# Moving the first steps of an attention between the last products of a Fourier stage

## The chip, the cores and the metric

The kernel runs on one core of one Trainium2 chip. The metric is the device time of one execution in microseconds (us), and lower is better. The engines are PE (TensorE, the matrix engine), ACT (ScalarE), DVE (VectorE), POOL (GpSimd) and SP, which only issues loads here. Each engine works through its own instructions in the order in which the program lists them, and waits for the others by semaphores.

## The reference, cut to what matters

The model is one block with a Fourier branch beside an attention branch, followed by a second block (retention, latent attention, feed-forward). The change touches only the end of the Fourier branch and the beginning of the first attention. What they compute is this:

```
def fourier_branch(f_in, w_fmix, b_fmix):
    f = f_in.reshape(b, l, 8, 64)
    fr = real(fftn(f, axes=(1, 3), norm='ortho'))
    return einsum('blgc,gcd->blgd', fr, w_fmix) + b_fmix     # times silu(f_gate)

def gqa_block(q_blk, k, v):
    s = einsum('bkgqd,bksd->bkgqs', q_blk, k) * HEAD_DIM ** -0.5
    p = softmax(s, axis=-1)
    return einsum('bkgqs,bksd->bkgqd', p, v)                 # times silu(a_gate)
```

There are 1024 tokens and 16 meta tokens (1040 keys), 8 query heads of 64 values and 2 key and value heads.

## The kernel before, in words

**Where the work lies.** PSUM, the memory into which PE writes, is used as four pairs of banks, A, B, C and Dp (the trace calls them psa, psb, psc and psd). A pair holds 2 x 512 values for each of 128 partitions. Tiles in the other on-chip memory stand at addresses that are written out by hand, so a tile may reuse the place of another that is dead.

**The Fourier stage** (`pe_fourier`, `act_fourier`, `dve_fourier`). It has two steps. First come five small blocks of 8 matmuls ("mixed"), which ACT copies to the tiles GA and GB. ACT then also makes the high parts of the keys for both heads (KHH), and DVE the low parts (KLL), since a float32 operand is worked on as a high and a low part. Then come eight products, called "four" 0 to 7, of 20 matmuls with 260 columns each (L793). Behind product n, ACT copies one of its two banks to QSB (`L816`), and DVE does four operations (L832, L837, L838, L842): it forms the difference and the sum of both banks in PSB and multiplies each into the gate tile GT. L832 and L838 read one operand from PSUM and one tile of the other memory; L837 and L842 read two tiles of the other memory. The products go round all four pairs.

**The first attention** (`pe_attention`, `act_attention`, `dve_attention`, `pool_attention`). It works on 64 units, u = 0 to 63, of 128 queries of one head against all keys; four units make a group g. Before the loop stand five steps that are done once: the values are turned to tokens x channels by 9 transposes into pairs C and Dp (`pe_values_in`, L858 and L859), ACT copies them to the tile VS1 as high parts and DVE forms the low parts (signal "v low"); DVE splits the first queries (`dve_stage_first`, L877 and L879, signal ("q", 0)); PE computes the scores of the first group against the 16 meta tokens into pair Dp (`pe_meta_scores`, 8 matmuls of 16 columns), ACT copies them out and DVE takes their maxima; and PE computes the scores of unit 0 (`pe_scores`, four matmuls of 512 columns into pair A; unit u uses pair A or B in turn). Then, for each unit, DVE takes the maximum over the keys (L1054) and makes the bias (L1056), ACT computes the exponentials (L991, then L995 for the meta tokens), DVE inverts the sum (`dve_norms`, L1062 and L1065), POOL multiplies the probabilities by it (L1106, L1107), PE turns them by 8 transposes into pair C (`pe_turns`, L940), ACT and DVE split these into high and low parts (PTH and PTL, L1004 and L1071), and PE multiplies them with the values, once for each group, into pair Dp (L962). The turning lags three units behind the scores. On PE the order of a step u is: turns of u-3, scores of u+1, a third of a group's value matmuls, and after every fourth unit the next group's meta scores. POOL also splits the next head's queries (L889 and L897, signal ("q", n)) and gates each group's output (L1136).

**What orders the work around the change.** The order on each engine is written out: `tensor_program` calls `pe_gate`, then `pe_fourier`, then `pe_attention`, and the other engines have the same sequence. The attention's one-time steps therefore wait for product 7 and for its last DVE operation: `pe_values_in` waits for ("four", 7), `act_values_in` for ("four gated", 7). POOL has nothing between its last weight split and unit 0.

Of the kernel before, what the change touches and what calls it, by code (L numbers as in the profile page):

```python
# [6 lines left out]
F32 = mybir.dt.float32  # L7
F32R = mybir.dt.float32r
# [105 lines left out]
def two_block_kernel(nc, xT, pT, pos, slabs, cols, squares, rope1, dft, wf, cd, outT):  # L114
    with ExitStack() as ctx:
# [53 lines left out]

        PTH = [at(f"pth{j}", [P, 8, HALF], F32R, 27 + 32 * j) for j in range(2)]  # L170
        PTL = [at(f"ptl{j}", [P, 8, HALF], F32R, 43 + 32 * j) for j in range(2)]
        PM = [at(f"pm{j}", [P, 4, META], F32, 91 + 0.25 * j) for j in range(2)]
        KHH = [at(f"khh{j}", [P, L], F32R, 137.5 + 8.25 * j) for j in range(2)]
        KLL = [at(f"kll{j}", [P, L], F32R, 141.625 + 8.25 * j) for j in range(2)]
        PMS = [at(f"pms{j}", [P, 4, 2 * META], F32R, (91.5, 203.5)[j]) for j in range(2)]
        PMX = [at(f"pmx{j}", [P, 4, 2 * META], F32, (91.5, 203.5)[j]) for j in range(2)]
        PMT = at("pmt", [2 * META, HALF], F32R, 108.5)
        VS1 = [at(f"vs1{j}", [P, 9, P], F32R, 92 + 4.625 * j) for j in range(2)]
        QST = [at(f"qst{j}", [P, T], F32R, (199, 101.25)[j]) for j in range(2)]
# [114 lines left out]
        def col(name, j=0, lo=0, hi=P):  # L294
            return COLS[lo:hi, COL[name] + j:COL[name] + j + 1]
# [448 lines left out]
        def dve_fold(e):  # L744
# [12 lines left out]
            t.then_inc(*vec.up("wbd"))  # L757

        def four_pair(n):
            return (A, B, C, Dp)[n % 4]  # L760

        def fourier_free(e, n):

            if n >= MT5 + 4:
                e.wait_ge(*vec.on(("four", n - 4 - MT5)))
            elif n >= 4:
                e.wait_ge(*acted.on(("mixed", n - 4)))
            elif n == 0:
                e.wait_ge(*vec.on(("gate", 7)))
                e.wait_ge(*vec.on("wbd"))  # L770

        def pe_fourier(e):
            for mt in range(MT5):
                w = min(P, NM - mt * P)
                p = four_pair(mt)
                fourier_free(e, mt)
                for a, F_ in enumerate((FE, FO)):
                    for ct in range(4):
                        t = e.matmul(PS[p][0:w, a, ct * P:ct * P + P], lhsT=F_[:, ct, mt * P:mt * P + w],
                                     rhs=WBD[:, a, ct, :], start=True, stop=True, skip_group_check=True)  # L780
                t.then_inc(*psum.up(("mixed", mt)))
            e.wait_ge(*acted.on(("mixed", MT5 - 1)))
            e.wait_ge(*landed["ct"].on("all"))
            e.wait_ge(*landed["st"].on("all"))
            for n in range(8):
                dt, h = divmod(n, 2)
                p = four_pair(MT5 + n)
                fourier_free(e, MT5 + n)
                c0, cn = h * (NL // 2), NL // 2
# [8 lines left out]
        def act_fourier(e):  # L798
            e.wait_ge(*vec.on(("gate", 7)))
            for mt in range(MT5):  # L800
                w = min(P, NM - mt * P)
                e.wait_ge(*psum.on(("mixed", mt)))
                e.activation(GA[0:w, mt, :], PS[four_pair(mt)][0:w, 0, :], ACT.Copy)
                e.activation(GB[0:w, mt, :], PS[four_pair(mt)][0:w, 1, :], ACT.Copy).then_inc(*acted.up(("mixed", mt)))
            for kv in range(2):
# [4 lines left out]
                e.activation(KHH[kv][rest, :], K1[mine, :], ACT.Copy).then_inc(*acted.up(("k both", kv)))  # L810
            for n in range(8):
                cn = NL // 2
                e.wait_ge(*psum.on(("four", n)))
                if n >= 1:
                    e.wait_ge(*vec.on(("four", n - 1)))
                e.activation(QSB[:, 0:cn], PS[four_pair(MT5 + n)][:, 1, 0:cn], ACT.Copy  # L816
                             ).then_inc(*acted.up(("four", n)))

        def dve_fourier(e):
            for kv in range(2):  # L820
# [3 lines left out]
                e.tensor_tensor(KLL[kv][rest, :], K1[mine, :], KHH[kv][mine, :], SUB).then_inc(*vec.up(("k low", kv)))  # L824
            for n in range(8):
                dt, h = divmod(n, 2)
                c0, cn = h * (NL // 2), NL // 2
                p = PS[four_pair(MT5 + n)]
                k0 = META - 1 if h == 0 else 0
                k1 = cn if h == 0 else cn - 1  # L830
                e.wait_ge(*acted.on(("four", n)))
                e.scalar_tensor_tensor(out=PSB[:, 0:cn], in0=p[:, 0, 0:cn], scalar=col("b_fmix", dt), in1=QSB[:, 0:cn],  # L832
                                       op0=ADD, op1=SUB).then_inc(*vec.up(("four minus", n)))
                r0 = c0 + 1 + k0 - META
                seg = GT[:, dt, r0:r0 + cn - k0]
                e.wait_ge(*vec.on(("four minus", n)))
                e.scalar_tensor_tensor(out=seg, in0=PSB[:, k0:cn], scalar=0.5, in1=seg, op0=MUL, op1=MUL)  # L837
                e.scalar_tensor_tensor(out=PSB[:, cn:2 * cn], in0=p[:, 0, 0:cn], scalar=col("b_fmix", dt),  # L838
                                       in1=QSB[:, 0:cn], op0=ADD, op1=ADD).then_inc(*vec.up(("four", n)))
                seg = GT[:, dt, T - (c0 + k1):T - (c0 + 1) + 1]  # L840
                e.wait_ge(*vec.on(("four", n)))
                e.scalar_tensor_tensor(out=seg, in0=PSB[:, cn + k1 - 1:cn - 1:-1], scalar=0.5, in1=seg,  # L842
                                       op0=MUL, op1=MUL).then_inc(*vec.up(("four gated", n)))

# [10 lines left out]
        def pe_values_in(e):  # L855
            e.wait_ge(*vec.on(("four", 7)))
            for kt in range(8):
# [3 lines left out]
        def act_values_in(e):  # L861
            e.wait_ge(*psum.on("v turned"))
            e.wait_ge(*vec.on(("four gated", 7)))
            for kv in range(2):
# [2408 lines left out]
```

## Time and profile before

| what | us |
|---|---|
| median of three runs | 2178.56 (2178.27 to 2182.41) |
| the profiled execution | 2179.39 |
| its span in the trace | 2177.6 |
| products 0 to 7, PE | 270.4 to 311.8 |
| the attention's one-time steps and first units until the first turning | 311.8 to 331.5 |
| the rest of the attention's units | 331.5 to about 555 |

Times of the trace count from the start of its span. A row of the timeline gives the start, the duration, the engine, the line of the kernel, the operation, what is written and what is read, and, in brackets, how long the engine had been idle before it and what released it. PEclk and the granted clock are the clock that TensorE was given, as a share of its full 2.4 GHz; 0.50 is the lower of its two levels, 1.2 GHz.

### The profile page before, as it was taken

To read this page: it belongs to the slowest core of one execution; us is meant where nothing else is said; L and a number is where in the kernel's file an instruction comes from. 1 tells how busy PE (TensorE), PEld (TensorE's weight loads), DVE (VectorE), ACT (ScalarE), POOL (GpSimd) and SP (SyncE) were. 2 spreads that over 40 slices of the span, in tenths; PEclk is the share of its full clock that TensorE was granted. 3 is DMA by queue.
4 is the path that set the end of the run, shared out by engine and by line. 5 is a ranking of instruction groups with operands and counts; after the bars stand their busy time and mean duration, and the time that the engine had idled before them with its cause. 6 is when DMAs were issued, how large, how long until landed. Compare 5 with 4: busy or idle time off the path is not lost.

```text
span 2177.6 us, 25594 instructions
## 1 busy us (share of the span) xinstructions
PE 1992.6 (92%) x9543; PEld 1638.3 (75%) x9543; DVE 1322.9 (61%) x1846; ACT 917.1 (42%) x1614; POOL 941.9 (43%) x658
## 2 busy tenths in 40 slices
PE   5999988999999999988888798789999999999878
PEld 5987757777778888866766686667888887787667
DVE  5354148998786354455545546577655568969735
ACT  4121217888532222245556544443333343445541
POOL 0333308888000000007566100479999995746030
PEclk9999989999999999989999999899999999999989
DMA  3112100000423111100000231323232238784202
GB/s 146 49 39 90 47 0 1 1 1 1 145 87 135 40 39 39 40 20 30 20 20 20 97 96 59 135 87 107 81 113 88 91 122 295 233 303 164 87 30 97
DMA packets 68412, 179.57 MB, mean 82 GB/s; under 512 B 6529, under 2 KB 8321, under 8 KB 68289
## 3 DMA queue, kind: packets, MB, share of 16 engines
q1 hardware_dynamic: 42624, 120.19, 16.9%
q10 hardware_dynamic: 25664, 57.74, 7.3%
q8 instruction: 77, 1.26, 0.3%
q14 instruction: 47, 0.38, 0.1%
HBM read 148.02 MB, written 29.88 MB: 82 GB/s over the span
## 4 chain that ended last, share of the span: by engine, by line
PE 28%; DVE 11%; issue 6%; ACT 5%; POOL 4%; DMA 0%; ACTq 0%; DVEq 0%; SPq 0%; POOLq 0%
PE psc L2432 4%; PE psa L2432 4%; PE psd L2432 3%; PE psb L2432 3%; PE psb L341 3%; PE psa L341 3%; POOL wrf L2298 3%; PE psd L341 2%; PE psd L1896 2%; PE psc L1859 1%; DVE bl L2594 1%; DVE blf L2580 1%; PE psc L341 1%; DVE tiny L1827 1%; POOL wrl L2316 1%
## 5 line engine op out<-in xcount | busy, mean ns | idle before, releaser
L2298 POOL TENSOR_TENSOR wrf<-wr 128x512 f32<-128x512 f32 x155 | 250.7, 1620 | 238.8 <-DMA wr<-slabs 231.6
L1848 POOL TENSOR_TENSOR lps<-lps,tiny 128x128 f32<-128x128 f32 (+2 forms) x24 | 14.7, 613 | 496.0 <-DVE tiny L1843 495.2
L2311 ACT ACTIVATE wrh<-wrf 128x512 fp32r<-128x512 f32 x155 | 97.6, 630 | 178.1 <-POOL wrf L2298 177.5
L2316 POOL TENSOR_TENSOR wrl<-wrf,wrh 128x512 fp32r<-128x512 f32 x111 | 165.6, 1499 | 11.4 <-ACT wrh L2311 11.4
L1106 POOL TENSOR_TENSOR pb<-pb,tiny 128x1024 f32<-128x1024 f32 x64 | 121.2, 1894 | 89.1 <-DVE tiny L1065 87.4
L341 PE MATMUL psb<-mh,wh 128*128 128x512 f32 x352 | 125.2, 400 | 4.1 <-issue 2.5
L364 ACT ACTIVATE wh<-wraw 128x1024 fp32r<-128x1024 f32 x82 | 86.1, 1053 | 92.5 <-PE psb L341 46.0
L370 DVE TENSOR_TENSOR wl<-wraw,wh 128x1024 fp32r<-128x1024 f32 x75 | 91.3, 1221 | 52.4 <-ACT wh L364 48.5
L341 PE MATMUL psb<-ml,wh 128*128 128x512 f32 x352 | 123.1, 394 | 0.0
L341 PE MATMUL psb<-mh,wl 128*128 128x512 f32 x352 | 122.9, 393 | 0.0
L2316 POOL TENSOR_TENSOR wrl<-wr,wrh 128x512 fp32r<-128x512 f32 x62 | 107.7, 1740 | 26.3 <-ACT wrh L2311 25.8
L353 POOL TENSOR_TENSOR wh<-wraw,one 128x1024 fp32r<-128x1024 f32 x16 | 30.3, 1893 | 188.8 <-PE psc L341 76.9
L341 PE MATMUL psa<-mh,wh 128*128 128x512 f32 x288 | 107.9, 411 | 4.3 <-issue 2.3
L341 PE MATMUL psa<-ml,wh 128*128 128x512 f32 x288 | 105.2, 401 | 4.9 <-DVE ml L2198 2.7
L341 PE MATMUL psa<-mh,wl 128*128 128x512 f32 x288 | 104.0, 397 | 0.0
L1071 DVE TENSOR_TENSOR ptl<-psc,pth 128x512 fp32r<-128x512 f32 x128 | 82.4, 685 | 20.2 <-ACT pth L1004 19.9
L1004 ACT ACTIVATE pth<-psc 128x512 fp32r<-128x512 f32 x128 | 69.7, 597 | 43.6 <-PE psc L940 43.5
L341 PEld LDWEIGHTS psb<-mh,wh 128*128 128x128 f32 x352 | 66.3, 191 | 18.3 <-issue 2.8
L1880 DVE TENSOR_TENSOR ltl<-psc,lth 128x512 fp32r<-128x512 f32 (+2 forms) x96 | 50.3, 550 | 47.2 <-ACT lth L1871 47.1
L341 PEld LDWEIGHTS psb<-mh,wl 128*128 128x128 f32 x352 | 67.0, 190 | 14.5
L940 PE MATMUL psc<-sqc,pb 128*128 128x128 f32 x512 | 69.3, 279 | 9.4 <-POOL pm L1107 8.8
L341 PEld LDWEIGHTS psb<-ml,wh 128*128 128x128 f32 x352 | 67.2, 191 | 14.0
(641 smaller groups left out, 5972.6 us busy)
## 6 DMA issues: line engine op xcount, KB each, us to landing
wraw<-slabs SPq DMA_DIRECT2D x98, 512.0 KB, 3.6
wr<-slabs SPq DMA_DIRECT2D x132, 256.0 KB, 4.3
wr<-slabs SPq DMA_DIRECT2D x40, 512.0 KB, 3.5
hidden<-hf ACTq DMA_DIRECT2D x22, 512.0 KB, 3.8
half_sums<-hsum ACTq DMA_DIRECT2D x22, 256.0 KB, 3.6
x<-xT SPq DMA_DIRECT2D x8, 520.0 KB, 10.1
h<-xT SPq DMA_DIRECT2D x8, 512.0 KB, 6.5
residual<-h ACTq DMA_DIRECT2D x8, 512.0 KB, 6.1
```

Source lines behind the costliest of these rows:

```text
L341: t = e.matmul(o, lhsT=lw, rhs=xx(kt, c0, cn), start=n == 0, stop=n == total - 1, skip_group_check=True)
L364: e.activation(WH[j][:, :], RAW[:, j, :], ACT.Copy).then_inc(*acted.up(("high", s)))
L370: e.tensor_tensor(WL[j][:, :], RAW[:, j, :], WH[j][:, :], SUB).then_inc(*vec.up(("split", s)))
L940: t = e.transpose(PS[C][:, h, kt * P:kt * P + P], PB[u % 4][:, c:c + P], SQC[:, 0, :])
L1004: e.activation(PTH[g % 2][:, 4 * h:4 * h + 4, v * P:v * P + P], PS[C][:, h, :].rearrange("p (k q) -> p k q", q=P), ACT.Copy).then_inc(*act ...
L1071: e.tensor_tensor(PTL[g % 2][:, 4 * h:4 * h + 4, v * P:v * P + P], PS[C][:, h, :].rearrange("p (k q) -> p k q", q=P), PTH[g % 2][:, 4 * h: ...
L1106: e.tensor_tensor(PB[v][:, :], PB[v][:, :], RI[:, v:v + 1].to_broadcast([P, T]), MUL)
L1880: t = e.tensor_tensor(LTL[:, k0:k1, v * P:v * P + P], PS[C][:, b, 0:(k1 - k0) * P].rearrange("p (k q) -> p k q", q=P), LTH[:, k0:k1, v * P ...
L2298: e.tensor_tensor(WRF[n % NW][:, :], x, y, WEIGHTS[product(n)][2]).then_inc(*pooled.up(("sum", n)))
L2311: e.activation(WRH[n % NW][:, :], x, ACT.Copy).then_inc(*acted.up(("high part", n)))
L2316: e.tensor_tensor(WRL[n % NW][:, :], x, WRH[n % NW][:, :], SUB).then_inc(*pooled.up(("low", n)))
L2432: t = e.matmul(o, lhsT=wt[n % NW][:, kt * P:kt * P + P], rhs=x, start=kt == 0 and pas == 0 and p not in (7, 6), stop=kt == 3 and pas == 2, ...
```

## The change

The five one-time steps are put between the products, on every engine. The eight products use pairs B and A in turn (0 to 5), then C (6) and Dp (7), so that C and Dp are free for the values and the meta scores. On PE the turning of the values stands before product 2, the meta scores of group 0 before product 5, and the scores of unit 0 before product 7; the scores of unit 1 follow product 7, which is where the loop has them. On DVE the first queries are split before product 0's operations. The operations behind product 7 move into the loop: on ACT behind the exponentials of unit 0, on DVE behind the maximum and the norm of unit 0. Some tiles get other addresses, since they now live beside CT, ST and QSB. No arithmetic is added or left out.

```
-            return (A, B, C, Dp)[n % 4]                         # four_pair
+            return (B, A)[n % 2] if n < 6 else (C, Dp)[n - 6]
         def fourier_free(e, n):
-            if n >= MT5 + 4:
-                e.wait_ge(*vec.on(("four", n - 4 - MT5)))
...
+            if n == 6:
+                e.wait_ge(*vec.on("v low"))
+            elif n == 7:
+                e.wait_ge(*acted.on(("meta s", 0)))
+            elif n >= 2:
+                e.wait_ge(*vec.on(("four", n - 2)))
...
             for n in range(8):                                  # pe_fourier
+                if n == 2:
+                    pe_values_in(e)
+                if n == 5:
+                    e.wait_ge(*acted.on(("k both", 1)))
+                    pe_meta_scores(e, 0)
+                if n == 7:
+                    e.wait_ge(*vec.on(("four", 5)))
+                    pe_scores(e, 0)
...
+            for n in range(7):                                  # act_fourier
+                act_four(e, n)
+                if n == 1:
+                    act_values_in(e)
+                if n == 4:
+                    act_meta_scores(e, 0)
...
+            dve_stage_first(e)                                  # dve_fourier
+            for n in range(7):
+                dve_four(e, n)
+                if n == 1:
+                    dve_values_in(e)
+                if n == 4:
+                    dve_meta_max(e, 0)
...
         def pe_values_in(e):
-            e.wait_ge(*vec.on(("four", 7)))
         def act_values_in(e):
-            e.wait_ge(*vec.on(("four gated", 7)))
         def pe_attention(e):
-            pe_values_in(e)
-            e.wait_ge(*vec.on("v low"))
-            e.wait_ge(*acted.on(("k both", 1)))
-            pe_meta_scores(e, 0)
-            pe_scores(e, 0)
         def act_attention(e):
-            act_values_in(e)
-            act_meta_scores(e, 0)
...
+                if u == 0:
+                    act_four(e, 7)                              # behind act_exps(e, 0)
         def dve_attention(e):
-            dve_values_in(e)
-            dve_stage_first(e)
-            dve_meta_max(e, 0)
...
-                if 0 <= u - 1 < NU:
+                if 0 < u - 1 < NU:
                     dve_norms(e, u - 1)
+                if u == 0:
+                    dve_norms(e, 0)
+                    dve_four(e, 7)
```

`act_four(e, n)` and `dve_four(e, n)` are the old loop bodies, made into functions. PTH, PTL, PM, PMS, PMX and VS1 change their addresses.

## Rows read from the trace of the kernel before

**Rows 1.** Page, part 1: busy us, share of the span, instructions

```profile
PE 1992.6 (92%) x9543; PEld 1638.3 (75%) x9543; DVE 1322.9 (61%) x1846; ACT 917.1 (42%) x1614; POOL 941.9 (43%) x658
```

**Rows 2.** Windows: stretch, length, PE, PEld, DVE, ACT, POOL busy, clock, DMA share, GB/s

```profile
270.30:311.80 41.50, 41.38 (x160) 27.67 (x160) 17.09 (x32) 6.92 (x12) 0.00 (x0) 1.00 0.00 0
311.80:331.50 19.70, 11.88 (x42) 9.26 (x42) 10.54 (x22) 5.49 (x15) 2.32 (x3) 0.57 0.00 0
331.50:344.88 13.38, 9.29 (x58) 6.93 (x57) 12.92 (x30) 10.77 (x30) 12.91 (x13) 0.97 0.01 2
344.88:351.27 6.39, 6.39 (x21) 5.19 (x22) 3.11 (x6) 2.58 (x6) 4.80 (x5) 0.52 0.00 0
357.81:371.40 13.59, 13.24 (x80) 10.87 (x80) 12.54 (x27) 11.04 (x27) 11.15 (x11) 1.00 0.01 1
```

**Rows 3.** Timeline, from the last product to the first turning

```profile
309.12 2.65 PE L793 MATMUL psa<-st,gb 128*128 128x260 f32 x10
311.81 0.39 ACT L816 ACTIVATE qsb<-psa 128x260 f32<-128x260 f32 x1 [4.77 <-PE psa L793]
312.23 0.49 DVE L832 SCALAR_TENSOR_TENSOR psb<-psa,cols,qsb 128x260 f32<-128x260 f32 x1 [3.36 <-ACT qsb L816]
313.61 0.43 DVE L842 SCALAR_TENSOR_TENSOR gt<-psb,gt 128x259 f32<-128x259 f32 x1
313.63 1.97 PE L858 MATMUL psc<-sqc,v 128*128 128x128 f32 x8 [1.87 <-DVE psb L838]
319.33 1.22 DVE L879 TENSOR_TENSOR qst<-q,qst 64x1024 fp32r<-64x1024 f32 x1
320.70 0.35 PE L913 MATMUL psd<-khh,qst 128*128 128x16 f32 x1 [4.88 <-DVE qst L879]
322.40 0.77 PE L928 MATMUL psa<-khh,qst 128*128 128x512 f32 x1
324.49 1.23 DVE L1054 TENSOR_REDUCE tiny<-psa 128x1 f32<-128x1024 f32 x1 [1.43 <-PE psa L929]
326.00 1.11 ACT L991 ACTIVATE pb<-psa,tiny 128x1024 f32<-128x1024 f32 x1 [3.19 <-DVE tiny L1056]
327.26 0.80 PE L928 MATMUL psa<-khh,qst 128*128 128x512 f32 x1 [1.10 <-ACT pb L991]
328.14 1.89 POOL L1106 TENSOR_TENSOR pb<-pb,tiny 128x1024 f32<-128x1024 f32 x1 [67.75 <-DVE tiny L1065]
331.25 1.89 POOL L1106 TENSOR_TENSOR pb<-pb,tiny 128x1024 f32<-128x1024 f32 x1 [1.04 <-DVE tiny L1065]
331.50 1.09 PE L940 MATMUL psc<-sqc,pb 128*128 128x128 f32 x8
```

**Rows 4.** Timeline: the second, third, fourth and fifth unit on POOL, and PE behind it

```profile
335.36 1.89 POOL L1106 TENSOR_TENSOR pb<-pb,tiny 128x1024 f32<-128x1024 f32 x1
335.84 0.16 DVE L1065 RECIPROCAL tiny<-tiny 128x1 f32<-128x1 f32 x1
342.76 1.89 POOL L1106 TENSOR_TENSOR pb<-pb,tiny 128x1024 f32<-128x1024 f32 x1
344.88 1.97 PE L940 MATMUL psc<-sqc,pb 128*128 128x128 f32 x8 [1.09 <-POOL pm L1107]
```

**Rows 5.** Timeline: meta scores and unit scores at the full clock, first and last

```profile
372.78 0.19 PEld L913 LDWEIGHTS psd<-khh,qst 128*128 128x128 f32 x1
373.71 0.26 PE L915 MATMUL psd<-kll,qst 128*128 128x16 f32 x1
```

**Rows 6.** DVE with two SBUF tiles (min/median/max ns), and POOL beside one of them

```profile
L1154 DVE TENSOR_TENSOR ml<-gt,mh x16: 678/681/1777, 555.2 to 566.2; 128x512 fp32r<-128x512 f32 x16
557.34 1.73 POOL L1136 TENSOR_TENSOR gt<-ot,gt 64x512 f32<-64x512 f32 x1 [5.74 <-DVE ot L1080]
```

**Rows 7.** Timeline: gating on POOL, one group in two, first and last

```profile
371.36 1.27 POOL L1136 TENSOR_TENSOR gt<-ot,gt 64x512 f32<-64x512 f32 x1 [0.17 <-POOL qst L897]
508.37 1.28 POOL L1136 TENSOR_TENSOR gt<-ot,gt 64x512 f32<-64x512 f32 x1 [0.17 <-POOL qst L897]
```

More of the change, by code:

```diff
@@ L168, in two_block_kernel @@
         PSB = at("psb", [P, NL], F32, 162.5)
[L170 to L172 removed]
+        PTH = [at(f"pth{j}", [P, 8, HALF], F32R, (27, 68.25)[j]) for j in range(2)]
+        PTL = [at(f"ptl{j}", [P, 8, HALF], F32R, (43, 84.25)[j]) for j in range(2)]
+        PM = [at(f"pm{j}", [P, 4, META], F32, 205.75 + 0.25 * j) for j in range(2)]
         KHH = [at(f"khh{j}", [P, L], F32R, 137.5 + 8.25 * j) for j in range(2)]
         KLL = [at(f"kll{j}", [P, L], F32R, 141.625 + 8.25 * j) for j in range(2)]
[L175 to L176 removed]
+        PMS = [at(f"pms{j}", [P, 4, 2 * META], F32R, (206.25, 203.5)[j]) for j in range(2)]
+        PMX = [at(f"pmx{j}", [P, 4, 2 * META], F32, (206.25, 203.5)[j]) for j in range(2)]
         PMT = at("pmt", [2 * META, HALF], F32R, 108.5)
[L178 removed]
+        VS1 = [at(f"vs1{j}", [P, 9, P], F32R, 59 + 4.625 * j) for j in range(2)]
         QST = [at(f"qst{j}", [P, T], F32R, (199, 101.25)[j]) for j in range(2)]
@@ L802, in act_fourier @@
                 e.wait_ge(*psum.on(("mixed", mt)))
-                e.activation(GA[0:w, mt, :], PS[four_pair(mt)][0:w, 0, :], ACT.Copy)
-                e.activation(GB[0:w, mt, :], PS[four_pair(mt)][0:w, 1, :], ACT.Copy).then_inc(*acted.up(("mixed", mt)))
+                e.activation(GA[0:w, mt, :], PS[mixed_pair(mt)][0:w, 0, :], ACT.Copy)
+                e.activation(GB[0:w, mt, :], PS[mixed_pair(mt)][0:w, 1, :], ACT.Copy).then_inc(*acted.up(("mixed", mt)))
             for kv in range(2):
@@ L810, in act_fourier, with act_four @@
                 e.activation(KHH[kv][rest, :], K1[mine, :], ACT.Copy).then_inc(*acted.up(("k both", kv)))
[L811 to L817, printed above, removed]
+            for n in range(7):
[4 more added lines that the diff above has]
+                    act_meta_scores(e, 0)
+        def act_four(e, n):
+            cn = NL // 2
+            e.wait_ge(*psum.on(("four", n)))
+            if n >= 1:
+                e.wait_ge(*vec.on(("four", n - 1)))
+            e.activation(QSB[:, 0:cn], PS[four_pair(n)][:, 1, 0:cn], ACT.Copy).then_inc(*acted.up(("four", n)))
         def dve_fourier(e):
@@ L824, in dve_fourier @@
                 e.tensor_tensor(KLL[kv][rest, :], K1[mine, :], KHH[kv][mine, :], SUB).then_inc(*vec.up(("k low", kv)))
[L825 to L843, printed above, removed]
@@ new lines, in dve_fourier, with dve_four @@
+            dve_stage_first(e)
[5 more added lines that the diff above has]
+                    dve_meta_max(e, 0)
+        def dve_four(e, n):
+            dt, h = divmod(n, 2)
+            c0, cn = h * (NL // 2), NL // 2
+            p = PS[four_pair(n)]
+            k0 = META - 1 if h == 0 else 0
+            k1 = cn if h == 0 else cn - 1
+            e.wait_ge(*acted.on(("four", n)))
+            e.scalar_tensor_tensor(out=PSB[:, 0:cn], in0=p[:, 0, 0:cn], scalar=col("b_fmix", dt), in1=QSB[:, 0:cn],
+                                   op0=ADD, op1=SUB).then_inc(*vec.up(("four minus", n)))
+            r0 = c0 + 1 + k0 - META
+            seg = GT[:, dt, r0:r0 + cn - k0]
+            e.wait_ge(*vec.on(("four minus", n)))
+            e.scalar_tensor_tensor(out=seg, in0=PSB[:, k0:cn], scalar=0.5, in1=seg, op0=MUL, op1=MUL)
+            e.scalar_tensor_tensor(out=PSB[:, cn:2 * cn], in0=p[:, 0, 0:cn], scalar=col("b_fmix", dt),
+                                   in1=QSB[:, 0:cn], op0=ADD, op1=ADD).then_inc(*vec.up(("four", n)))
+            seg = GT[:, dt, T - (c0 + k1):T - (c0 + 1) + 1]
+            e.wait_ge(*vec.on(("four", n)))
+            e.scalar_tensor_tensor(out=seg, in0=PSB[:, cn + k1 - 1:cn - 1:-1], scalar=0.5, in1=seg,
+                                   op0=MUL, op1=MUL).then_inc(*vec.up(("four gated", n)))
```

18 lines of the change are left out of this document (9 added, 9 removed).

## The prediction, as it was put on record before the changed kernel was run

> **What bounds the kernel now.** I read the page first. PE is busy for 92% of the span, far above the other engines [rows 1], so a gain must come from a stretch in which PE is idle or slow. The windows by stage show such a stretch exactly where the diff works [rows 2]. During the products PE is busy for 41.4 of 41.5 us at the full clock. In the 19.7 us after them it is busy for 11.9, at a mean granted clock of 0.57, while no other engine is busy for more than 10.5. In the next 13.4 us POOL is busy for 12.9, and only from about 351 us on does a group of four units take the 13.6 us of the steady loop.
>
> The timeline of the 19.7 us is one chain with one thing running at a time [rows 3]. The last product ends at 309.12 + 2.65 = 311.77. ACT and four DVE operations follow, to 314.04. The turning of the values has just begun, at 313.63, and at half speed (1.97 us; the same form takes 1.09 at the full clock, the last row of the group). Value parts and query parts follow on ACT and DVE until 320.55. PE, idle for 4.88 us, then does meta scores from 320.70 and unit 0's scores from 322.40, both at the low clock. DVE's maximum starts at 324.49, the exponentials at 326.00, POOL's first unit at 328.14 and its second at 331.25. From there POOL paces the stage: with query splits between them its third unit starts at 335.36 and its fifth at 342.76, and PE waits for it at 344.88 [rows 3, 4].
>
> So the second unit on POOL (331.25) is the mark to follow: 331.25 - 311.77 = 19.48 us after the last product.
>
> **The change part by part.**
>
> *Two pairs for six products.* Product n now waits for ("four", n-2). DVE signals it at its third operation, about 2 us after product n-2 ends (312.23 to 313.61 is all that comes before the fourth), and product n starts 5.2 us after that end, with product n-1 between. Over 3 us of slack: cost 0. If another product's operations were late by more than that, each us would be paid on PE.
>
> *PE work put between the products.* Nine transposes: 1.09 for eight plus about 0.1 [rows 3]. Meta scores at the full clock: 372.78 to 373.71 + 0.26, of which about 1.0 delays the next instruction [rows 5]. Scores of unit 0: at the low clock 322.40 to 324.49 = 2.1 at most, so about 1.0 at the full one [rows 3]. Since PE has no pause there, it keeps the full clock. Sum 3.1 us, bounds 2.9 and 5.9 (the latter with 2.1, 1.7 and 2.1 at the low clock [rows 3], which needs a pause that I don't find). Product 7 then ends at 314.87.
>
> *Value copies, value low parts, meta copy and maxima, first query split.* ACT and DVE were busy for 6.9 and 17.1 of the 41.5 us [rows 2]. These steps take some 2 us on ACT and 5 on DVE and lie under 5.2 us products. The query split (about 2 us) delays DVE's operations behind product 0; product 2 needs those only after product 1 and the transposes, 2 us later than DVE has them. Cost 0. If this cover went, what is late next would be product 2, by at most the 2 us.
>
> *Unit 0 before product 7.* Its scores are there about 1 us after product 6. DVE does the operations of product 6 (to about 311), the maximum and the bias; ACT's exponentials start near 312.5 and POOL's first unit near 314.6, all under product 7. The new wait on DVE is the norm of unit 0 ahead of product 7's operations: behind it are queued those operations, unit 1's maximum and everything after. It is met near 314.0, before product 7 ends. Cost 0; bound 0.5.
>
> *Product 7's tail.* This is the new critical chain. Product 7 ends at 314.87. ACT and DVE end 2.27 later (314.04 - 311.77 in rows 3), at 317.14. Then unit 1's maximum and bias, 326.00 - 324.49 = 1.51; then from exponential to POOL's unit, 328.14 - 326.00 = 2.14 [rows 3].
>
> *Contention, new.* Two of product 7's DVE operations read two tiles of the ordinary memory (L837, L842), and POOL is now multiplying unit 0 (1.89 us) beside them. Before, POOL was idle throughout the products [rows 2]. The trace has the same meeting elsewhere: a DVE operation on two such tiles takes 0.68 us alone and up to 1.78 where POOL's gating runs beside it, and POOL's gating then takes 1.73 in place of 1.27 [rows 6, 7]. Bounds 0 and 2 x 1.1 = 2.2; POOL's unit ends near 316.7, so only the first of the two meets it. I take 0.6.
> The Trainium skill, GPSIMD Engine Reference, section 1 Specifications, says that GpSimd's SBUF interfaces are shared with VectorE and contend with its instructions that have two SBUF inputs. By that rule the chain gets longer by this term; without it the gain would be 0.6 us larger.
>
> So POOL's second unit starts at 314.87 + 2.27 + 0.6 + 1.51 + 2.14 = 321.39, against 331.25: **9.9 us earlier**.
>
> *What is late next: PE.* Unit 2's scores run right behind unit 1's, near 315.9, but unit 3's need pair B, that is unit 1's exponentials: 319.25 + 1.26 = 320.51 (1.26 from 326.00 and 327.26 in rows 3). PE is idle for over 3 us before, so I take the low clock: 1.8 for the scores, 1.7 for the meta scores of group 1, and the first turning starts at 324.0, only 7.5 us earlier than at 331.50. POOL's fourth unit needs unit 3's norm, which came at 335.84 + 0.16, 4.5 us after the first turning [rows 3, 4]: 328.5. POOL could take it at 335.36 + 2.03 - 9.86 = 327.5. Delay about 1.1 us with the start; bounds 0 (the clock stays up) and 2.5. POOL's fifth unit moves from 342.76 to 334.0: 8.8 us earlier.
>
> *The second low stretch.* From 344.88 to 351.27 PE ran at 0.52 and took 6.39 us for a step that takes 13.59 / 4 = 3.4 in the steady loop [rows 2]: 3.0 lost, after two pauses in which PE waited for POOL. The pauses stay, since POOL still paces there, so I expect it again. It may be shorter or be missed: bounds 0 and 3.0 us of further gain; I take 0.6.
>
> *After that* the steady loop runs at its own rhythm (10 groups in 508.37 - 371.36 = 137.0 us [rows 7]), and the later stages follow on waits, not on a fixed time. The moved tiles have the same shapes: 0. No DMA is issued at another place of any queue; POOL's queue only waits for "v low" earlier.
>
> Sum: 9.9 - 1.1 + 0.6 = **9.4 us**. The profiled execution took 2179.39 (span 2177.6, so 1.8 around it): 2170.0. It lies 0.8 above the median of the runs, 2178.56, so the predicted median is 2169.2.
>
> **The rivals.**
>
> *The low stretch goes.* If PE's pauses before the turning of unit 4 fall differently, it runs on at the full clock: gain 8.8 + 3.0 = 11.8, 2166.8. For it: those pauses were only about 1 us each (1.09 in the row at 344.88), so little decides. Against it: PE has, if anything, more time to wait there than before.
>
> *The low clock stays.* After the pause before 320.5 the clock could stay down. From the first turning at 324.0, four turnings (1.65), four scores (1.8) and a set of meta scores (1.7) take 15.5 us, so unit 4's turning starts at 339.5, 5.4 us earlier than 344.88: 2173.2. Against it: in rows 2 the stretch from 331.50, with similar pauses, stood at 0.97.
>
> *The gain is given back.* The attention ends earlier, but pauses and clock drops of the later stages fall differently by a few us. The three runs differ by 4.1 us. Gain under 4.4 us: about 2176.
>
> *Slower: the loop settles in another rhythm.* The steady loop is closed over PE, ACT, DVE and POOL, with PE busy 13.24 of 13.59 us, DVE 12.54 [rows 2]. It now starts with unit 0 and 1 much further apart. If the order in which DVE meets its waits locked into a longer period, each of 15 groups would pay. It decides from 9.4 / 15 = 0.63 us a group; with 1.0 us the kernel loses 15.0 - 9.4 = 5.6 and takes 2184.2. Against it: 13.59 for the second group and 13.70 over the next ten [rows 2, 7], although the loop now starts from a disturbed state too.
>
> *The change doesn't do what it says* if a wait in the middle, ("four", 5) or "v low", holds up PE: each us there would be lost one for one. The slack found above speaks against it; I put it into the cases of small gain.
>
> **How the numbers follow.** Forecast (gain 7.5 to 10.5) 0.50; low stretch gone 0.26; clock stays low 0.12; given back or held up 0.09; slower 0.03. 0.2% is 4.4 us, about what a measurement of this kernel can tell from no change. The first three lie beyond it: 0.88, and a little of the fourth: faster 0.89, same 0.08, slower 0.03. The range reaches from the second case with half a us beyond its centre to the third with a little: 2165.6 to 2173.6.
>
> **What would show it.** The last product ends near 314.9 with no PE pause over 0.5 us since 270.4, and the clock is 1.00 throughout. One of L837 and L842 of product 7 takes clearly more than 0.43 us. POOL's second unit starts near 321.4, its fifth near 334.0. The fourth starts after a wait for DVE of about 1 us. A clock near 0.5 stands around the turning of unit 4. Groups still take 13.6 to 13.7 us. The forecast is wrong if PE pauses between the products, if POOL's fifth unit moves by less than 7 or more than 10.5 us, or if the end moves by another amount than the loop.

## The result, and the profile after

The changed kernel takes 2168.61 us (median of 5 runs, 2166.19 to 2171.67), the kernel before 2178.97 (5 runs, 2178.27 to 2182.41): a ratio of 0.995, 95% interval 0.9938 to 0.9963. The forecast was 2169.2, range 2165.6 to 2173.6; by the medians the gain is 10.4 us, where 9.4 was forecast. The profiled execution took 2168.61, its span 2166.7, which is 10.9 us less than before. PE does the same number of matmuls and is busy for 3.0 us less than before [rows 1], so 3.0 of the 10.9 were slow time of PE and the rest was idle time:

```profile
PE 1989.6 (92%) x9543; PEld 1635.3 (75%) x9543; DVE 1322.0 (61%) x1846; ACT 917.0 (42%) x1614; POOL 941.2 (43%) x658
```

Both executions reach product 0 at slightly different times (270.39 and 269.53), so from here on marks are counted from its first matmul. The windows of the changed kernel, with the columns of [rows 2]: the products with what now lies between them, then all up to the turning of unit 7, then parts of it.

```profile
269.45:313.66 44.21, 44.13 (x182) 30.32 (x182) 22.40 (x43) 9.89 (x21) 0.33 (x1) 1.00 0.00 0
313.66:345.54 31.88, 25.99 (x134) 20.96 (x134) 26.67 (x55) 21.77 (x54) 23.87 (x24) 0.89 0.00 1
314.00:319.00 5.00, 1.70 (x8) 1.05 (x6) 4.75 (x8) 1.29 (x4) 1.58 (x2) 1.00 0.01 2
319.00:322.40 3.40, 3.35 (x13) 2.97 (x13) 1.84 (x5) 1.66 (x6) 2.52 (x3) 0.53 0.00 0
322.40:326.00 3.60, 3.60 (x14) 3.11 (x15) 1.96 (x6) 2.46 (x6) 3.51 (x3) 0.50 0.01 2
335.43:345.54 10.11, 10.11 (x58) 8.20 (x58) 8.96 (x20) 7.85 (x19) 8.74 (x10) 1.00 0.01 2
```

PE has no pause between the products (44.13 busy of 44.21) and keeps the full clock. Behind product 7 it pauses for over 3 us, and the clock is at its lower level from just after 319 to about 326. Such a time at the lower level is called a low stretch below. Around the turning of unit 4, where [rows 2] has 0.52, it is now 1.00.

The timeline of the changed kernel along the chain, to be laid beside [rows 3, 4]: last product, DVE's operations behind it (L861 to L871), unit 1's maximum (L1076) and exponentials (L1013), POOL's units (L1128), the turnings (L967).

```profile
311.00 2.65 PE L807 MATMUL psd<-st,gb 128*128 128x260 f32 x10
313.33 1.89 POOL L1128 TENSOR_TENSOR pb<-pb,tiny 128x1024 f32<-128x1024 f32 x1 [53.80 <-DVE tiny L1087]
313.69 0.39 ACT L837 ACTIVATE qsb<-psd 128x260 f32<-128x260 f32 x1 [0.95 <-PE psd L807]
314.63 0.88 DVE L866 SCALAR_TENSOR_TENSOR gt<-psb,gt 128x260 f32<-128x260 f32 x1
315.94 0.43 DVE L871 SCALAR_TENSOR_TENSOR gt<-psb,gt 128x259 f32<-128x259 f32 x1
316.29 1.21 DVE L1076 TENSOR_REDUCE tiny<-psb 128x1 f32<-128x1024 f32 x1
317.79 1.11 ACT L1013 ACTIVATE pb<-psb,tiny 128x1024 f32<-128x1024 f32 x1 [3.71 <-DVE tiny L1078]
319.05 0.67 PE L955 MATMUL psb<-khh,qst 128*128 128x512 f32 x1 [3.34 <-ACT pb L1013]
319.80 1.90 POOL L1128 TENSOR_TENSOR pb<-pb,tiny 128x1024 f32<-128x1024 f32 x1 [4.22 <-DVE tiny L1087]
322.35 1.97 PE L967 MATMUL psc<-sqc,pb 128*128 128x128 f32 x8
327.94 1.89 POOL L1128 TENSOR_TENSOR pb<-pb,tiny 128x1024 f32<-128x1024 f32 x1 [1.95 <-DVE tiny L1087]
333.30 1.89 POOL L1128 TENSOR_TENSOR pb<-pb,tiny 128x1024 f32<-128x1024 f32 x1
335.43 1.09 PE L967 MATMUL psc<-sqc,pb 128*128 128x128 f32 x8 [1.06 <-POOL pm L1129]
345.54 1.09 PE L967 MATMUL psc<-sqc,pb 128*128 128x128 f32 x8
```

The marks of all profiled executions, each read from a timeline as here and with the start of its product 0 taken off (us). POOL's units are counted from 0, so "its second unit" is the column 1 and "its fifth" the column 4. POOL gates the output of 16 groups (L1136 of the kernel before), and "last gating" is the start of the last. The last two columns tell where the clock fell later: the time from the seventh gating to the ninth, near the middle of the attention, and between the last two. The repeat of the changed kernel has a low stretch that these columns don't show: between its 14th and 15th gating lie 6.73 us, and 5.15 to 5.18 in the eleven others.

| kernel | product 7 ends | POOL unit 0 | 1 | 3 | 4 | turning 4 | turning 7 | last gating | middle | end |
|---|---|---|---|---|---|---|---|---|---|---|
| before | 41.38 | 57.75 | 60.86 | 67.00 | 72.37 | 74.49 | 87.42 | 286.95 | 27.14 | 7.02 |
| changed | 44.12 | 43.80 | 50.27 | 58.41 | 63.77 | 65.90 | 76.01 | 278.77 | 28.73 | 8.60 |
| changed, again | 44.13 | 43.80 | 50.28 | 57.95 | 63.32 | 65.44 | 75.55 | 276.76 | 27.16 | 7.03 |
| values only | 42.31 | 54.01 | 57.12 | 63.26 | 68.63 | 70.75 | 83.62 | 283.20 | 27.15 | 7.03 |
| tail first | 43.21 | 48.98 | 52.14 | 58.88 | 64.24 | 66.36 | 76.48 | 277.60 | 28.71 | 7.02 |
| both units | 45.05 | 43.80 | 47.08 | 58.50 | 63.86 | 65.98 | 76.10 | 276.66 | 27.15 | 8.36 |
| POOL waits | 44.12 | 46.48 | 49.83 | 57.10 | 62.47 | 64.59 | 74.71 | 275.84 | 27.13 | 8.59 |
| PE kept busy | 44.14 | 43.81 | 50.29 | 56.44 | 61.81 | 63.93 | 74.05 | 275.24 | 27.15 | 8.62 |
| waits and busy | 44.13 | 46.49 | 49.85 | 56.00 | 61.37 | 63.49 | 75.13 | 276.28 | 28.72 | 7.02 |
| both, spread | 45.04 | 43.79 | 47.07 | 56.16 | 61.53 | 63.66 | 73.77 | 273.10 | 27.14 | 7.03 |
| spread and busy | 45.05 | 43.80 | 47.08 | 54.53 | 59.89 | 62.01 | 72.13 | 272.97 | 27.14 | 8.59 |
| before, busy | 41.37 | 57.32 | 60.43 | 66.58 | 71.97 | 74.09 | 84.20 | 286.93 | 28.72 | 8.59 |

From before to changed the chain is ahead by 10.6 us at POOL's second unit, by 8.6 at its fifth, by 11.4 at the turning of unit 7 (no low stretch there any more) and by 8.2 at the last gating: 1.6 us went in a low stretch in the middle of the attention and 1.6 at its end, which the profiled execution of before did not have. The repeat of the changed kernel is ahead by 10.2 at the last gating, since it has only one of the two. With 0.86 ahead of product 0 and 1.9 behind the attention that makes the 10.9 us between the spans.

### The profile page after: what moved, and what is told of

Its sections match the earlier page's. It is cut to its first block, busy times and chain, and to the rows that moved or that the text cites. A ratio compares the mean times of both kernels' runs of the same rounds, so it can differ in the third digit from the quotient of the medians.

```text
span 2166.7 us, 25593 instructions
## 1 busy us (share of the span) xinstructions
PE 1989.6 (92%) x9543; PEld 1635.3 (75%) x9543; DVE 1322.0 (61%) x1846; ACT 917.0 (42%) x1614; POOL 941.2 (43%) x658
## 4 chain that ended last, share of the span: by engine, by line
PE 29%; DVE 11%; issue 5%; ACT 5%; POOL 4%; DMA 0%; ACTq 0%; DVEq 0%; SPq 0%; POOLq 0%
PE psa L2454 4%; PE psc L2454 4%; PE psb L2454 3%; PE psb L341 3%; PE psa L341 3%; PE psd L2454 3%; POOL wrf L2320 2%; PE psd L341 2%; PE psd L1918 2%; DVE bl L2616 1%; PE psc L341 1%; PE psc L1881 1%; DVE tiny L1849 1%; DVE blf L2602 1%; ACT lp L1859 1%
## 5 line engine op out<-in xcount | busy, mean ns | idle before, releaser
L1128 POOL TENSOR_TENSOR pb<-pb,tiny 128x1024 f32<-128x1024 f32 x64 | 121.2, 1894 | 79.1 <-DVE tiny L1087 77.6
L1902 DVE TENSOR_TENSOR ltl<-psc,lth 128x512 fp32r<-128x512 f32 (+2 forms) x96 | 50.2, 549 | 47.4 <-ACT lth L1893 47.2
L967 PE MATMUL psc<-sqc,pb 128*128 128x128 f32 x512 | 69.8, 280 | 8.8 <-POOL pm L1129 7.2
```

The lines of the kernel that those rows point to most:

```text
L967: t = e.transpose(PS[C][:, h, kt * P:kt * P + P], PB[u % 4][:, c:c + P], SQC[:, 0, :])
L1128: e.tensor_tensor(PB[v][:, :], PB[v][:, :], RI[:, v:v + 1].to_broadcast([P, T]), MUL)
L1902: t = e.tensor_tensor(LTL[:, k0:k1, v * P:v * P + P], PS[C][:, b, 0:(k1 - k0) * P].rearrange("p (k q) -> p k q", q=P), LTH[:, k0:k1, v * P ...
```

## The experiments

The experiments were run in three groups, each on one chip together with the kernel before, and each ratio is against that kernel's runs beside it (medians 2178.95, 2179.09 and 2177.83). The changed kernel ran only in the first result and, as its repeat, in the second group. Where lines are left out of a diff, "..." stands.

**Values only.** Query split, meta scores and unit 0's scores are put back behind product 7, and so ACT and DVE work on product 7 ahead of unit 0 again.

```
-                if n == 5:                                   # pe_fourier
-                    e.wait_ge(*acted.on(("k both", 1)))
-                    pe_meta_scores(e, 0)
-                if n == 7: ...
-            dve_stage_first(e)                               # dve_fourier
...
         def dve_attention(e):
+            dve_stage_first(e)
+            dve_meta_max(e, 0)
...
```

> Of the change, only the value turning (PE before product 2, ACT and DVE behind product 1) and the two pairs stay; query split, meta scores and unit 0's scores go back behind product 7. Times count from the start of product 0. My theory (what is gained is the time of the one-time steps in the chain behind the last product, each at its own length): the chain loses transposes, value copies and value low parts, which stood between 314.04 and the query split at 318.63, and product 7 ends 1.1 us later: POOL's second unit comes near 57.4 (before 60.9, changed kernel 50.3), and the time is some 3.5 us below before, about 2175.5. Rival 1 (the gain is the clock: PE without its pause keeps 1.00): the pause behind product 7 is still there, so the clock falls as before and nearly nothing is gained, 2178. Rival 2 (the pairs do it): nearly all of the gain is there, 2169.

Measured: POOL's second unit at 57.12 (expected 57.4), the last gating 3.75 us earlier than before; behind the turning of unit 7 neither execution has a low stretch. The median of 10 runs is 2176.85 (2171.36 to 2182.0), ratio 0.9991 (0.998 to 1.0001), so the time itself doesn't resolve it; the marks do. By them both rivals fall: moving the value steps brings their own length less what PE pays (3.7 us at POOL's second unit), although the pause and the low clock stay and although the pairs are the changed ones.

**Tail first.** Unit 0's scores follow product 7, and the operations behind product 7 come before unit 0 on ACT and DVE.

```
-                if n == 7:                                   # pe_fourier
-                    e.wait_ge(*vec.on(("four", 5)))
-                    pe_scores(e, 0)
...
+            e.wait_ge(*vec.on(("four", 5)))                  # pe_attention
+            pe_scores(e, 0)
...
```

> The changed kernel, but unit 0's scores stand behind product 7 and the operations behind product 7 come first on ACT and DVE, as in the kernel before. Values, queries and meta scores stay between the products. My theory: units 0 and 1 then both wait for DVE's tail of product 7; product 7 ends 1.0 earlier, near 43.1 from product 0's start; POOL's first unit near 49 (changed kernel 43.8) but its second near 51.4 to 52 (50.3), so only 1 to 2 us of the gain is lost: about 2170. Rival (unit 0 under product 7 is what brings the gain): the first unit's 5 us are lost in full, about 2174.

Measured: units at 48.98 (49 expected) and 52.14 (51.4 to 52); the fifth at 64.24 (changed 63.77, its repeat 63.32) and the turning of unit 7 at 76.48 (76.01 and 75.55); 2171.34 us, ratio 0.9954 (0.994 to 0.9968). Putting unit 0 under product 7 starts POOL 5.2 us sooner. Of that 1.9 us are left at its second unit and 0.5 to 0.9 us from the fifth on, where PE has taken over. The rest of the gain is the one-time steps.

**Both units before product 7.**

```
                     pe_scores(e, 0)                          # if n == 7
+                    pe_scores(e, 1)
...
+                if u == 2:                                   # pe_attention
+                    e.wait_ge(*vec.on(("four", 7)))
...
```

ACT and DVE have unit 1's exponentials, maximum and norm ahead of the operations behind product 7. Also, POOL's first query split waits for the end of product 7, which came 4.4 us before it here.

> The changed kernel with unit 1's scores also before product 7, the exponentials and maxima of both units before the operations behind product 7, and one tile moved by 0.25 KB. Theory: product 7 ends 1.0 later (45.1 from product 0's start), POOL's second unit starts right behind its first, near 45.9 in place of 50.3, its third near 51.4 in place of 54.4, its fifth near 59.8 in place of 63.8; both gating operations of product 7 now meet POOL (about 0.9 us each in place of 0.43). Time 3 to 4 us under the changed kernel's 2168.6: about 2165. Rival: POOL's third unit is held by unit 2's maximum, which stands behind product 7's tail in any case, and the later units by PE, so that nothing is gained: 2168.6 or, with the extra 1.0 on PE, 2169.6.

Measured: 2170.97 us, ratio 0.9961 (0.9946 to 0.9976). The second unit came at 47.08 (45.9 expected), the third at 55.15 (51.4 expected, changed kernel 54.39), the fifth at 63.86: nothing gained. In the timeline of this kernel L867 and L872 are product 7's gating on DVE, and the row of PE is unit 3's first:

```profile
316.61 1.89 POOL L1132 TENSOR_TENSOR pb<-pb,tiny 128x1024 f32<-128x1024 f32 x1 [1.21 <-DVE tiny L1090]
316.94 1.84 DVE L867 SCALAR_TENSOR_TENSOR gt<-psb,gt 128x260 f32<-128x260 f32 x1
319.00 1.89 POOL L917 TENSOR_TENSOR qst<-q,one 64x1024 fp32r<-64x1024 f32 x1
319.21 1.96 DVE L872 SCALAR_TENSOR_TENSOR gt<-psb,gt 128x259 f32<-128x259 f32 x1
319.24 0.80 PE L956 MATMUL psb<-khh,qst 128*128 128x512 f32 x1 [3.53 <-DVE psb L868]
321.10 1.21 DVE L1079 TENSOR_REDUCE tiny<-psa 128x1 f32<-128x1024 f32 x1
```

Each gating operation lasts until 0.28 us after the POOL operation beside it: 1.84 and 1.96 us in place of 0.43. That is twice the 0.9 that I had put down. It ate the whole lead of 3 us together with my own wait on ("four", 7) in front of unit 3's scores; the spread kernel below takes both away at once, so their shares are not told apart.

**POOL waits.** POOL's first unit waits for product 7's gating.

```
         def pool_attention(e):
-            e.wait_ge(*vec.on("v low"))
+            e.wait_ge(*vec.on(("four gated", 7)))
```

> The changed kernel, but POOL starts unit 0 only when product 7's gating on DVE is through, so that they don't meet. Theory (the 0.88 us of product 7's first gating operation, against 0.42 elsewhere, is POOL's doing): that operation takes 0.42, product 7's tail is 0.45 us shorter, POOL's unit 0 starts 2.5 us later at 46.4 from product 0's start, its second unit 0.45 earlier at 49.8; the time falls by 0.5 at most. Rival (POOL's first unit is what the stage waits for): all moves later by 2.5 us, 2171. Second rival: the 0.88 stays, so it comes from something else.

Measured: the gating operation took 0.43 us in place of 0.88,

```profile
315.15 0.43 DVE L866 SCALAR_TENSOR_TENSOR gt<-psb,gt 128x260 f32<-128x260 f32 x1
316.52 1.89 POOL L1128 TENSOR_TENSOR pb<-pb,tiny 128x1024 f32<-128x1024 f32 x1 [56.48 <-DVE gt L871]
319.12 0.50 PE L955 MATMUL psb<-khh,qst 128*128 128x512 f32 x1 [2.91 <-ACT pb L1013]
```

POOL's second unit came at 49.83 (50.27), although its first came 2.7 us later; 2168.95 us, ratio 0.9949 (0.9934 to 0.9964), the time of the changed kernel. So the 0.45 us are POOL's doing, and POOL's first unit has slack. The later marks are 1.3 us earlier than in the changed kernel and 0.85 earlier than in its repeat, both more than the 0.45: unit 3's scores took their first matmul at the full clock here (0.50 against 0.67), since the clock fell 0.6 us later than in the changed kernel (by windows of 1 us, at 50.3 from product 0's start against 49.7). In the repeat it fell at 50.2, and there the scores only started later. The Trainium skill, GPSIMD Engine Reference, section 1 Specifications, has GpSimd's SBUF interfaces shared with VectorE, with contention for instructions with two SBUF inputs; the trace agrees, 0.43 against 0.88, 1.84 and 1.96 us.

**PE kept busy.** Extra matmuls, read by nothing, between the scores of units 2 and 3.

```
+                if u == 2:                                   # pe_attention
+                    for _ in range(14):
+                        e.matmul(PS[C][:, 0, :], lhsT=QST[0][:, 0:P], rhs=KHH[0][:, 0:HALF], ...)
```

> The changed kernel with 14 extra matmuls of unit 0's scores into the free pair C, whose results nothing reads, between unit 2's and unit 3's scores on PE, where it paused for 3.3 us (315.7 to 319.05). Theory (the clock falls because of that pause, and the low stretch of about 6 us behind it is a term of the sum): the granted clock stays at 1.00 from product 0 to the first turnings, unit 3's scores take 0.95 in place of 1.7, the first turning starts 1.6 earlier (51.2 in place of 52.8 from product 0's start), POOL's fourth unit 57.1 in place of 58.4 and its fifth 62.5 in place of 63.8; time 1 to 1.5 us under 2168.6. Rival (POOL paces there, so PE's clock costs nothing): POOL's fifth unit stays at 63.8.

Measured, in windows of this kernel:

```profile
313.00:319.00 6.00, 6.00 (x27) 4.45 (x26) 4.48 (x9) 1.34 (x6) 2.26 (x2) 1.00 0.00 1
319.00:322.00 3.00, 2.86 (x19) 2.27 (x18) 2.21 (x5) 2.56 (x9) 1.52 (x1) 1.00 0.00 0
322.00:326.00 4.00, 3.65 (x22) 2.53 (x20) 3.84 (x12) 3.76 (x9) 3.84 (x4) 1.00 0.01 2
```

The clock stays at 1.00, POOL's second unit at 50.29 is unmoved, its fourth comes at 56.44 (58.41) and its fifth at 61.81 (63.77; 63.32 in the repeat). So the pause behind product 7 costs 1.5 to 2.0 us through the clock. The first turning came at 51.36 (51.2 expected). The time, 2168.91 (0.9954, 0.9934 to 0.9973), shows none of it, with runs that spread over 8 us. The marks keep it: the lead over the repeat is 1.5 us at the turning of unit 7 and 1.5 at the last gating, each execution having one low stretch near the end (8.62 in the last column here; one gating earlier in the repeat). The Trainium skill, TensorE: Matmul & The Clock Gate, section "What's actually happening", has the throttled clock as the default which activity releases; keeping PE active removed the low stretch here, so the trace agrees.

**Both, spread.** Both units before product 7, the wait on ("four", 7) only before the meta scores, the operations behind product 7 after unit 2's maximum, and the two gating operations in units 7 and 9.

```
...
-                if u == 1:                                   # dve_attention
-                    dve_four(e, 7)
+                if u == 2:
+                    dve_four(e, 7)                           # without its two gating operations
+                if u == 7: ...                               # the first of them
+                if u == 9:
+                    dve_four_gate(e, 7)
...
```

> As the run with both units before product 7, with its two faults taken away: PE waits for product 7's reading only before the meta scores, not before unit 3's scores, and DVE's two gating operations of product 7 (1.84 and 1.96 us there, beside POOL) stand in units 7 and 9 instead of ahead of unit 2's maximum. Theory (what ate the gain there was DVE's tail, at 4.75 us in place of 1.8): POOL's second unit stays at 47.1 from product 0's start, its third comes near 50.6 (changed kernel 54.4), its fifth near 59 (63.8), the first turning near 50.6 (52.8); the two gating operations still take up to 1.9 each, later, and give back 0 to 2; time 3 to 5 us under the changed kernel. Rival (POOL's third unit is held by something else than the tail): it stays near 54.

Measured: 2164.87 us (4 runs, 2163.99 to 2167.47), ratio 0.9926 (0.9907 to 0.9946), beside 2169.6 of the changed kernel on the same chip, 0.9942 (0.9922 to 0.9963). Its median is the lowest here. Its tail and the gating operations, with POOL beside them:

```profile
316.61 1.90 POOL L1147 TENSOR_TENSOR pb<-pb,tiny 128x1024 f32<-128x1024 f32 x1 [1.21 <-DVE tiny L1098]
317.82 0.48 DVE L862 SCALAR_TENSOR_TENSOR psb<-psd,cols,qsb 128x260 f32<-128x260 f32 x1
318.22 0.48 DVE L869 SCALAR_TENSOR_TENSOR psb<-psd,cols,qsb 128x260 f32<-128x260 f32 x1
333.10 1.90 POOL L1147 TENSOR_TENSOR pb<-pb,tiny 128x1024 f32<-128x1024 f32 x1
334.24 1.04 DVE L1131 SCALAR_TENSOR_TENSOR gt<-psb,gt 128x260 f32<-128x260 f32 x1
341.10 0.41 DVE L880 SCALAR_TENSOR_TENSOR gt<-psb,gt 128x259 f32<-128x259 f32 x1
341.27 2.00 POOL L1147 TENSOR_TENSOR pb<-pb,tiny 128x1024 f32<-128x1024 f32 x1
```

The two operations with an operand in PSUM (L862, L869) took 0.48 us beside POOL. The gating operation that started while POOL was at work ended 0.28 us after it; the other started 0.17 us ahead of POOL's and took 0.41. The third unit came at 51.26 (50.6 expected), the fifth at 61.53, not 59: PE waited 1.7 us for product 7's reading and its clock fell to 0.50. By the marks it is 1.8 us ahead of the changed kernel's repeat at turning 7 and 3.7 at the last gating, where the repeat has lost 1.6 in a low stretch and this kernel has not. The two intervals overlap, so the 4.7 us between the medians are not resolved.

**Waits and busy.** POOL waits and PE has the extra matmuls.

> POOL waits for product 7's gating, and PE has the 14 extra matmuls. Theory: the two effects add up only in part, since in the run where POOL waits the clock fell late (320.3) anyway: POOL's second unit 49.8 from product 0's start, fourth 56.9, fifth 62.3 (62.47 with the wait alone, 63.77 in the changed kernel); time some 1.5 us under the changed kernel. Rival (both cost nothing): the time of the changed kernel.

Measured: units at 49.85, 56.00 and 61.37, so each 0.44 us earlier than in the busy kernel, which is the contention alone. A low stretch at the turning of unit 4 then took 1.5 us (turnings 4 and 7 are 11.6 us apart in place of 10.1). 2168.44 (2163.83 to 2177.26), ratio 0.9947 (0.9932 to 0.9962): the time of the changed kernel.

**The changed kernel again.**

> The changed kernel itself, for comparison on the same chip: 2168.6, with 43.8, 50.3 and 63.8 us from product 0's start to POOL's first, second and fifth unit. Whether the low stretch at the turning of unit 4 is there is open; where it is, the later units come up to 3 us later. If these marks differ from the first execution by more than 0.1 us up to the second unit, differences that small between the other runs mean nothing.

Measured: 2169.6, ratio 0.9942 (0.9922 to 0.9963). Marks agree within 0.01 us up to POOL's second unit. Behind the pause they differ by 0.45, since the clock fell at another moment (49.7 and 50.2 from product 0's start). So of the later marks, differences of half a us between executions mean nothing unless the clock is the same.

**Before, kept busy.** Four extra matmuls in each of PE's last two pauses ahead of unit 4's turning.

```
+                if u == 7:                                   # ahead of pe_turns
+                    for _ in range(4):
+                        e.matmul(PS[Dp][:, 1, :], lhsT=QST[0][:, 0:P], rhs=KHH[0][:, 0:HALF], ...)
+                if u == 6: ...                               # the same ahead of pe_meta_scores
```

> The kernel before the change, with 4 extra matmuls of 512 columns in each of the two pauses of PE ahead of unit 4's turning (before group 2's meta scores and before the turning), whose results nothing reads. Theory (the low stretch of 6.4 us at 0.52 behind those pauses comes from them and costs 3.0 us): the clock stays at 1.00 there, the turning of unit 7 starts at about 84.4 us from product 0's start in place of 87.4, everything up to unit 4 on POOL (72.4) stays, and the time falls by up to 3, to 2176. Rival (the clock falls from an earlier pause, or at random): the low stretch stays, and with it 2179.

Measured, windows of this kernel against the 0.52 of [rows 2]:

```profile
340.00:345.00 5.00, 4.94 (x31) 3.93 (x31) 4.38 (x11) 2.89 (x8) 4.92 (x4) 1.00 0.02 3
345.00:350.00 5.00, 5.00 (x31) 4.27 (x30) 3.65 (x8) 3.82 (x9) 4.61 (x5) 1.00 0.00 0
```

The low stretch is gone and turning 7 comes 3.2 us earlier (84.20), of which 0.4 was there at POOL's first unit already. That leaves 2.8 us for the stretch. But the last gating is at 286.93, as before: the middle and the end of the attention had low stretches of 1.6 us each in this execution. The median of 10 runs is 2179.04 (2173.54 to 2186.62), ratio 1.0007 (0.9991 to 1.0023). The local price is shown in one pair of executions; that filling the pauses shortens the kernel is not.

**Spread and busy.** Seven extra matmuls where the spread kernel's PE waited 1.7 us.

> The kernel with both units before product 7 and spread gating, plus 7 extra matmuls on PE where it waited 1.7 us before the first meta scores of the loop. Theory: the clock stays at 1.00 there, the first turning starts near 49.3 from product 0's start in place of 50.6, POOL's fourth unit near 54.5 in place of 56.2 and its fifth near 60; time about 1.5 us lower, 2163.4. Rival (the clock costs nothing there, or the extra matmuls delay as much as they save): 2164.9 or more.

Measured: fourth unit at 54.53 and fifth at 59.89 as expected, and the clock at 1.00; the first turning at 50.14, later than the 49.3 expected. 2166.76 (6 runs, 2164.19 to 2172.7), ratio 0.9953 (0.9938 to 0.9967), no better than without (2164.87), so by the time the rival stands; the two kernels ran on different chips. By the marks the 1.6 us of lead at turning 7 met a low stretch at the end (8.59 against 7.03).

## Why the prediction was right, point by point

The time lay 0.6 us from the forecast, and most steps hold in the trace, but one did not, and the total hides it. By the prediction's own signs this counts against its account: no clock near 0.5 stood around the turning of unit 4, and the end moved by another amount (10.9 us) than the loop (11.4 at the turning of unit 7, 8.2 at the last gating). A slip in its range changes nothing: the low end, 2165.6, lies 1.2 us below the second rival's 2166.8 and not half a us.

*Work between the products*: 44.12 - 41.38 = 2.74 us on PE, forecast 3.1, with no pause and the full clock. The new waits and the ACT and DVE steps cost nothing, as said.

*Product 7's tail and contention*: from the end of product 7 (313.65) to unit 1's maximum (316.29) 2.64, forecast 2.27 + 0.6. The contention term was 0.45, on the first gating operation only; taking the meeting away removed just that. Maximum to exponentials 1.50 (1.51), exponentials to POOL 2.01 (2.14). POOL's second unit: gain 10.6, forecast 9.9.

*PE is late next*: unit 3's scores waited for unit 1's exponentials, the clock fell, the first turning came at 52.82 (forecast 53.6). POOL then waited 1.95 us for unit 3's norm (forecast 1.1). Its fifth unit came at 63.77, forecast 63.6. The busy kernel shows the cause: with the clock up, the wait is gone.

*The second low stretch*: this step failed. I took the stretch to recur around the turning of unit 4, because "the pauses stay" and PE has "if anything, more time to wait there". It occurred in neither execution of the changed kernel, and the pauses had not stayed. The kernel before, with what [rows 4] has at 344.88:

```profile
337.49 1.09 PE L940 MATMUL psc<-sqc,pb 128*128 128x128 f32 x8 [1.54 <-POOL pm L1107]
340.31 2.38 POOL L897 TENSOR_TENSOR qst<-q,qst 64x1024 fp32r<-64x1024 f32 x1
342.74 0.28 PE L913 MATMUL psd<-khh,qst 128*128 128x16 f32 x1 [1.00 <-POOL qst L897]
```

and the changed kernel, with 335.43 above:

```profile
328.60 1.17 PE L967 MATMUL psc<-sqc,pb 128*128 128x128 f32 x8 [0.70 <-DVE ptl L1093]
330.86 2.37 POOL L924 TENSOR_TENSOR qst<-q,qst 64x1024 fp32r<-64x1024 f32 x1
331.48 1.16 PE L967 MATMUL psc<-sqc,pb 128*128 128x128 f32 x8 [0.79 <-DVE ptl L1093]
333.41 0.17 PE L940 MATMUL psd<-khh,qst 128*128 128x16 f32 x1
```

Before, PE paused 1.54, 1.00 and 1.09 us, the 1.00 for POOL's query split ahead of group 2's meta scores. Changed, it paused 0.70, 0.79 and 1.06: measured against POOL it is later (unit 3's turning starts 1.8 us ahead of POOL's fifth unit, before 3.1), and it reaches the meta scores only at 333.41, when the split is over (333.23). That gave about 3 us more, the rival's case (gain 11.4 at turning 7, against 11.8 there). The other executions fit. The two with pauses of 1.5, 1.0 and 1.1 us there have the full stretch (before, values only). Seven have at most 0.8, 0.8 and 1.1, and none of them has it. Of the two between (0.9, 0.7 to 0.8, 0.4 and 1.1), waits and busy has a short one and PE kept busy none. In the kernel before with the last two pauses filled it is gone. Each is one execution, so this speaks for the pauses as the cause without giving a rule for them.

*What followed*: I wrote that the loop runs at its own rhythm. It does, but low stretches of 1.3 to 1.6 us fall on some executions in the middle (4 of 12) and near the end (7 of 12) and not on others, in changed and unchanged kernels alike. The pause in the middle is in all three executions of the two kernels, the kernel before, the changed one and its repeat in this order, but the clock fell only behind the second, whose turning took 1.53 us:

```profile
457.23 1.09 PE L940 MATMUL psc<-sqc,pb 128*128 128x128 f32 x8 [1.41 <-POOL pm L1107]
445.00 1.53 PE L967 MATMUL psc<-sqc,pb 128*128 128x128 f32 x8 [1.39 <-POOL pm L1129]
446.69 1.09 PE L967 MATMUL psc<-sqc,pb 128*128 128x128 f32 x8 [1.42 <-POOL pm L1129]
```

Near the end all three have pauses of 1.71 and 2.39 us; the clock fell behind the second in the changed kernel, behind the first in the repeat and behind neither in the kernel before. The profiled execution of the changed kernel had both low stretches, which gave back what the missing one had brought. That the forecast came so close is partly this, and that part is luck. Other rivals: the clock did not stay low, the loop's period did not change (27.1 us for two groups in most executions), no wait held up the products.

*What stays open*: from the last gating to the end of the span it takes 1620.3 us before and 1618.4 in the changed kernel, but 1621.1 in its repeat and 1618.4 to 1624.7 over all twelve. So the 1.9 us by which the rest was shorter lie within the scatter between executions; what makes it was not looked into.

## What to carry to other kernels

Steps that run one after another on different engines between two dense stages are worth their whole latency when they are moved under the dense stage, and cost only their own time on its engine (here 2.7 us for 10.6). The first item of a pipelined loop is worth moving only as far as the second and third can follow it: follow the chain of the item that paces the loop, and look there for operations that meet GpSimd with two SBUF inputs. A gain of 2 us found mark by mark can be real and still not show in medians whose executions differ by low stretches of 1.3 to 3 us; compare marks, and name the stretches.

## What the runs showed of the hardware

A VectorE operation with two SBUF inputs that meets a GpSimd tensor_tensor already at work does not share: in all four cases here it ended 0.28 to 0.29 us after the GpSimd operation (0.43 us alone, 0.88, 1.04, 1.84 and 1.96 beside it). I had not expected it to be all or nothing at this size. One that started 0.17 us ahead of the GpSimd operation took 0.41, and the GpSimd one 2.00 in place of 1.89. With one operand in PSUM it took 0.48 beside GpSimd, as long as alone. And PE's clock fell after pauses of 1.4 to 2.4 us in some executions and not after the same pauses in others of the same kernel; filling a pause with matmuls that nothing reads kept it at 1.00 at the filled place in all four kernels that tried it, while the low stretches of the other places came and went.
